# A two-block transformer kernel on one core: the output stages round both weight halves first, two modulation vectors change their place and one its engine

## The reference

```python
# second block, x: 256 x 2048
m = jax.nn.silu(c) @ w_ada + b_ada           # w_ada: 2048 x 6*2048
sh_a, sc_a, g_a, sh_m, sc_m, g_m = split(m)  # and the same of c_ctx for the context
h  = rms_norm(x, norm_attn_w) * (1 + sc_a) + sh_a
hc = rms_norm(ctx, norm_attn_w) * (1 + csc_a) + csh_a
...                                          # keys and values of hc and h, queries, pooling
x = x + g_a * (concat([attn, pool]) @ w_out)
hm = rms_norm(x, norm_mlp_w) * (1 + sc_m) + sh_m
x = x + g_m * (square(relu(hm @ w_up)) @ w_down)
return rms_norm(x, final_norm_w)
```

## Time and profile before

| what | value |
|---|---|
| time before, median of 3 runs | 1773.1 us (1772.69 to 1774.19) |
| the profiled execution | 1774.28 us |
| its span, first to last instruction | 1772.4 us |
| mean granted TensorE clock | 0.971 |
| PE busy | 1635.3 us, 92% |
| DVE busy | 1165.5 us, 66% |
| ACT busy | 768.3 us, 43% |
| raw loads | 496 of 512 KB |
| `w_ada` loads | 64 from SP, 32 from ACT, 1024 KB each |

### The profile page before, as it was taken

The page is one execution under the profiler, slowest core; times in us unless marked ns, Lnnn a source line. Parts: engine busy times, 40 slices in busy tenths (PEclk is TensorE's granted clock), DMA queues, the critical chain, the costliest instruction groups (busy, mean ns, idle before and its releaser), DMA issues.

```text
span 1772.4 us, 33734 instructions
## 1 busy us (share of the span) xinstructions
PE 1635.3 (92%) x12254; PEld 1501.3 (85%) x12254; DVE 1165.5 (66%) x1798; ACT 768.3 (43%) x1067; POOL 32.0 (2%) x49
## 2 busy tenths in 40 slices
PE   3799999899969977998989889999999999999996
PEld 3799998799968867877878879989998999899985
DVE  4577776688885557576755566656665666566675
ACT  4344443344433334444434445434543454345542
POOL 0000000000000000000000010000000000000000
PEclk9899999899989999999999989999999999999998
DMA  7688787688848765762224445555555556555552
GB/s 298 245 277 293 282 289 243 233 318 334 318 169 323 277 242 186 296 254 92 76 84 152 147 151 184 185 188 189 180 188 189 188 179 187 189 184 186 180 190 92
DMA packets 88120, 374.74 MB, mean 211 GB/s; under 512 B 9985, under 2 KB 10513, under 8 KB 75233
## 3 DMA queue, kind: packets, MB, share of 16 engines
q1 hardware_dynamic: 82224, 335.97, 55.3%
q10 hardware_dynamic: 4608, 33.56, 5.2%
q0 software_dynamic: 1200, 4.02, 0.7%
HBM read 371.40 MB, written 2.10 MB: 211 GB/s over the span
## 4 chain that ended last, share of the span: by engine, by line
issue 71%; DVE 12%; PE 11%; ACT 5%; DVEq 1%; POOL 0%; ACTq 0%; POOLq 0%
DVE lo L1088 5%; ACT hi L755 2%; PE G L396 2%; PE G L397 2%; PE G L398 2%; PE ADA L438 1%; PE M L636 1%; ACT sq L934 1%; DVE sqsum L1088 1%; DVE blk L1088 1%; PE S L610 1%; DVE sm L1413 1%; PE S L623 1%; PE ADA L650 1%; ACT actA L946 0%
## 5 line engine op out<-in xcount | busy, mean ns | idle before, releaser
L1088 DVE TENSOR_TENSOR lo<-raw,hi 128x1024 fp32r<-128x1024 f32 x496 | 607.8, 1225 | 326.1 <-ACT hi L755 316.0
L755 ACT ACTIVATE hi<-raw 128x1024 fp32r<-128x1024 f32 x496 | 526.1, 1061 | 488.1 <-PE G L398 276.4
L396 PE MATMUL G<-actA,hi 128*128 128x256 f32 (+1 forms) x2368 | 685.2, 289 | 20.1 <-DVE actA L1088 19.5
L397 PE MATMUL G<-actA,lo 128*128 128x256 f32 (+1 forms) x2368 | 672.5, 284 | 0.0
L398 PE MATMUL G<-actA,hi 128*128 128x256 f32 x2368 | 672.2, 284 | 0.0
L396 PEld LDWEIGHTS G<-actA,hi 128*128 128x128 f32 x2368 | 452.8, 191 | 54.5 <-issue 39.7
L397 PEld LDWEIGHTS G<-actA,lo 128*128 128x128 f32 x2368 | 452.4, 191 | 0.4
L398 PEld LDWEIGHTS G<-actA,hi 128*128 128x128 f32 x2368 | 451.6, 191 | 0.0
L422 PE MATMUL G<-actB,hi 128*128 128x512 f32 x1024 | 355.2, 391 | 0.0
L423 PE MATMUL G<-actB,lo 128*128 128x256 f32 x1024 | 287.2, 281 | 0.0
L422 PEld LDWEIGHTS G<-actB,hi 128*128 128x128 f32 x1024 | 191.6, 187 | 41.4
(11 more groups left out here) (186 smaller groups left out, 1102.1 us busy)
## 6 DMA issues: line engine op xcount, KB each, us to landing
raw<-stream_dram SPq DMA_DIRECT2D x496, 512.0 KB, 3.5
ada_raw<-w_ada_dram SPq DMA_DIRECT2D x64, 1024.0 KB, 6.7
ada_raw<-w_ada_dram ACTq DMA_DIRECT2D x32, 1024.0 KB, 6.4
x_tok<-x_tok_dram SPq DMA_DIRECT2D x1, 2048.0 KB, 8.2
resid<-xT_dram SPq DMA_DIRECT2D x1, 2048.0 KB, 11.7
ctx_tok<-ctx_tok_dram SPq DMA_DIRECT2D x1, 2048.0 KB, 18.5
W<-ctxT_dram POOLq DMA_DIRECT2D x16, 128.0 KB, 5.5
out_dram<-resid SPq DMA_DIRECT2D x4, 512.0 KB, 2.6
```

What stands on the lines that cost most here:

```text
L396: pe.matmul(wide, hi[:, slot, cols], x[:, k, 0:T + extra], start=(k == 0), stop=False, skip_group_check=True)
L397: pe.matmul(wide, lo[:, slot, cols], x[:, k, 0:T + extra], start=False, stop=False, skip_group_check=True)
L755: return act.activation(dst, src, ACT.Copy)
L1088: return dve.tensor_tensor(dst, a, b, op)
```

## The change

**ScalarE's order in the output stages.** In `out_body` the rounding of a unit's second half moves from the end of the unit's work to directly behind the first half. `ada_copy` of `sc_m` behind the first output stage goes.

**`sc_m`.** Its 16 tiles leave the first output stage and take the place that `g_m` had in key and query units, three of them earlier: one behind each of the units `U_KV+1` to `U_KV+7`, four in each of the pairs s = 0 and 1, one in s = 2. The table `SCALE_LOADS` places their loads. ACT copies the sums at the end of pair 2, where it was in pair 3. The turn and the addition that stood in the key units go.

**`g_m`.** PE has no tiles of it any more. DVE sums it in the down units of the MLP's groups 0 and 1: behind every second unit one multiply-add of 128x2048 (`scalar_tensor_tensor` into `gate_part`), 16 in all, from the two slots of `ada_raw`. SP loads each tile as 128x4x512 out of four column blocks (runs of 2 KB in place of 8 KB), and behind each such load the next four halves of weights. PE sums over the partitions ahead of group 3 with 16 matmuls (`gate_sums`), and DVE adds the bias. POOL clears `gate_part` after the first unit of the second output stage.

The diff, cut to its core:

```diff
+SCALE_LOADS = {U_KV + 2: 1, U_KV + 3: 1, U_KV + 4: 1, U_KV + 5: 1, U_KV + 6: 1, U_KV + 7: 2,
+               U_Q: 2, U_Q + 1: 2, U_Q + 2: 2, U_Q + 3: 1}
...
+    "dve gate down": {"seq": 4, "lo_done": 8, "gate_taken": 2},
...
         diag, adas = W[:, 3328:3584], W[:, 3584:4096]
+        gate_part = W[:, 1024:3072]
+        gate_c = cpad[:].rearrange("p k n -> p (k n)")
         ctx_raw = W[:, 0:1024].rearrange("p (s t) -> p s t", s=4)
...
                     ada_load(4 * KT + 1, 1, ada_taken, 2 * KT)
-                elif U_OUT1 <= u < U_KV - 2:
-                    e = u - U_OUT1 + 2
-                    ada_load(4 * KT + e, e % 2, ada_used, 2 * KT + e - 1)
                 weight(2 * u % RING, 2 * u + 8)
                 weight((2 * u + 1) % RING, 2 * u + 9)
-            ada_load(5 * KT, 0, ada_used, 3 * KT)
-            ada_load(5 * KT + 1, 1, ada_used, 3 * KT)
             e = 2
             for u in range(U_KV, U_OUT2):
-                for _ in range(1 if U_KV + 4 <= u < U_Q else 2 if U_Q <= u < U_Q + 6 else 0):
-                    if e < KT:
-                        ada_load(5 * KT + e, e % 2, ada_used, 3 * KT + e - 1)
-                        e += 1
+                for _ in range(SCALE_LOADS.get(u, 0)):
+                    ada_load(4 * KT + e, e % 2, ada_used, 2 * KT + e - 1)
+                    e += 1
                 weight(2 * u % RING, 2 * u + 8)
                 weight((2 * u + 1) % RING, 2 * u + 9)
-            with sp.Fori(0, (2 * UNITS - 2 * U_OUT2 - 8) // RING) as i:
-                for j in range(RING):
-                    weight(j, i * RING + 2 * U_OUT2 + 8 + j)
+            def weights(first, last):
+                with sp.Fori(0, 2 * (last - first) // RING) as i:
+                    for j in range(RING):
+                        weight(j, i * RING + 2 * first + 8 + j)
+            def gate_load(k):
+                m, g = divmod(k, 4)
+                src = ada_w[5 * KT:6 * KT].rearrange("(n m) p (g c) -> m g p n c", m=4, g=4)[m, g]
+                if k > 1:
+                    sp.wait_ge(gate_taken, 1 * (k - 1))
+                sp.dma_start(ada_raw[:, k % 2], src).then_inc(gate_full[k % 2], 16)
+            at = U_OUT2
+            for g in range(2):
+                weights(at, U_MLP + 2 * KT * g + KT)
+                if g == 0:
+                    sp.wait_ge(pool_ready, 4)
+                    gate_load(0)
+                for i in range(8):
+                    if 8 * g + i + 1 < KT:
+                        gate_load(8 * g + i + 1)
+                    at = U_MLP + 2 * KT * g + KT + 2 * i
+                    for n in range(2 * at + 8, 2 * at + 12):
+                        weight(n % RING, n)
+                at += 2
+            weights(at, UNITS - 4)
...
-            pool.wait_ge(ada_used, 4 * KT)
+            pool.wait_ge(ada_used, 2 * KT + KT)
             pool.dma_start(pool_w, t_in["pool_w"]).then_inc(pool_in, 16)
+            pool.wait_ge(w_used, 2 * U_OUT2 + 2)
+            pool.memset(gate_part, 0.0).then_inc(gate_zero, 1)
             power(14)
...
             for n in range(UNITS_OUT):
-                unit(At(U_OUT1), n, actB, inB, ada=2 * KT + n)
+                half_unit(At(U_OUT1), n, 0, actB, inB)
+                if n == 0:
+                    ada_turn()
+                half_unit(At(U_OUT1), n, 1, actB, inB)
                 if n == 1:
...
             broadcast()
             half_unit(at, 1, 1, actC)
+            ada_rows(2 * KT)
             unit(at, 2, actC)
-            ada_turn()
+            ada_rows(2 * KT + 1)
             unit(at, 3, actC)
+            ada_rows(2 * KT + 2)
             turn_values(y2[:, 0], U_KV + 3, 8)
             unit(at, 4, actA, inA, KT)
-            ada_rows(3 * KT)
+            ada_rows(2 * KT + 3)
             turn_values(y2[:, 1], U_KV + 4, 9)
             unit(at, 5, actA)
-            ada_rows(3 * KT + 1)
+            ada_rows(2 * KT + 4)
             pe.wait_ge(blk2_in, 64)
             rotate(y2[:, 0], U_KV + 5)
             unit(at, 6, actA)
-            ada_rows(3 * KT + 2)
+            ada_rows(2 * KT + 5)
             rotate(y2[:, 1], U_KV + 6)
             unit(at, 7, actA)
-            ada_rows(3 * KT + 3)
+            ada_rows(2 * KT + 6)
             turn_values(y2[:, 0], U_KV + 7, 10)
...
-                    pe.wait_ge(ada_added, 3 + 1)
+                    pe.wait_ge(ada_added, 2 + 1)
...
                 if s < 3:
-                    ada_rows(3 * KT + 4 + 4 * s)
-                    ada_rows(3 * KT + 5 + 4 * s)
+                    ada_rows(2 * KT + 7 + 4 * s)
+                if s < 2:
+                    ada_rows(2 * KT + 8 + 4 * s)
                 half_unit(at, 2 * s + 1, 0, actA)
...
                 half_unit(at, 2 * s + 1, 1, actA)
-                if s < 3:
-                    ada_rows(3 * KT + 6 + 4 * s)
-                    ada_rows(3 * KT + 7 + 4 * s)
+                if s < 2:
+                    ada_rows(2 * KT + 9 + 4 * s)
+                    ada_rows(2 * KT + 10 + 4 * s)
...
+            def gate_sums():
+                pe.wait_ge(gate_taken, KT)
+                for m in range(KT):
+                    x = pe.matmul(S[0][:, m:m + 1], gate_part[:, m * P:(m + 1) * P], ones[:, 0:1], start=(m == 0), stop=(m == KT - 1),
+                                  skip_group_check=True)
+                x.then_inc(gate_summed, 1)
...
                 base = U_MLP + 2 * KT * g
+                if g == MLP_GROUPS - 1:
+                    gate_sums()
                 if g == 0:
...
                     split(at, j, 0)
+                    split(at, j)
                     if ctx_too:
...
                     square(at, j, (sq[:, j % 2:j % 2 + 1], resid[:, u]))
-                    split(at, j)
...
                 out_body(At(U_OUT1, 4, i), i, True)
-            ada_copy(2)
...
                 split(at, 2 * s + 1)
+                if s == 2:
+                    ada_copy(2)
                 if s == 0:
...
-                    ada_add(3, 5)
+                    ada_add(2, 4)
...
                     dve.wait_ge(acc_zero, 1)
-                if g < MLP_GROUPS - 1:
+                if g < 2:
+                    if g == 0:
+                        dve.wait_ge(gate_zero, 1)
+                    with turn.lap(dve, 4, "dve gate down") as i:
+                        for j in range(4):
+                            down(At(base + KT, 4, i), j, bass.ds(i * 4 + j, 1), True, None)
+                            if j % 2:
+                                slot = j // 2
+                                dve.wait_ge(gate_full[slot], i * 16 + 16 * (4 * g + 1))
+                                dve.scalar_tensor_tensor(gate_part, ada_raw[:, slot].rearrange("p k n -> p (k n)"),
+                                                         gate_c[:, bass.ds(i * 76 + (8 * 38 * g + 38 * slot + 6), 1)], gate_part,
+                                                         ALU.mult, ALU.add).then_inc(gate_taken, 1)
+                                own(gate_taken)
+                elif g < MLP_GROUPS - 1:
                     with turn.lap(dve, 8, "dve down") as i:
...
                 else:
+                    dve.wait_ge(gate_summed, 1)
+                    seq(tt(adav[:, 0, G_M:G_M + KT], S[0][:, 0:KT], col("b_ada", 5 * KT, KT), ALU.add))
                     with turn.lap(dve, 7, "dve last down") as i:
```

More of the change, by code:

```diff
@@ L237, in program @@
         inP = sem("inP")
+        gate_zero, gate_taken, gate_summed = (sem(n) for n in ("gate_zero", "gate_taken", "gate_summed"))
+        gate_full = [sem(f"gate_full{i}") for i in range(2)]
         out_ready, out_sent = sem("out_ready"), sem("out_sent")
@@ L1010, in _ @@
                     value_copy(V2[:, :, P:T], 12)
-                if s == 3:
-                    ada_copy(3)
                 if s:
@@ L1395, in _ @@
                 split(at, n, 0)
-                if n == 4:
-                    ada_add(2, 4)
                 split(at, n)
```

## The result

The changed kernel takes **1722.8 us** (median of 5, 1722.0 to 1726.5) beside 1772.7 of the kernel before: ratio 0.972, 95% interval 0.971 to 0.974. The forecast was 1714 in a range of 1707 to 1726. The direction and nearly all of the gain are there; 8 to 9 us are missing. The profiled execution took 1722.0 us, its span is 1719.9, its mean granted clock 0.976.

The account below looks back on a forecast made before the run. PE is full nearly everywhere, but in both output stages ACT and DVE waiting for each other hold it. -35.2 - 4.5 - 22.9 + 3.5 = -59.1 gives 1715.2, taken as 1714 us; range 1707 to 1726, held 8 in 10.

Parts of the forecast that it names:

- Part 1: First output stage: ScalarE's new order and 16 tiles gone bring the first key unit's sums to 623.4, -35.2 us.
- ring: Output stages: ACT and DVE wait for each other once a unit, in laps of 7.65 and 6.88 us.
- the wait of 5.54: First key unit: PE stands 5.54 us for the last context tile; forecast to go.
- Part 2: Key and query units: moving the `sc_m` tiles there gives -4.5 us, at worst -2.
- the turn in pair 3: Query units: PE's 2.33 us wait there for ACT's copy goes, as the copy comes a unit earlier.
- Part 3: Second output stage: ScalarE's new order gives 5.75 us a unit and sums at 1007.0, -22.9 us.
- Part 4: MLP down units: `g_m` multiply-adds on VectorE of 2.33 us cost 0; PE's `gate_sums` cost +3.5 us.
- Part 5: Down units: gate loads cost 0, taking 2 KB runs at half a 4 KB run, DMA share 0.90.
- 1 MB ahead of it adds 3.3 at 300 GB/s: Down units: a weight load landing in 3.5 us is delayed 3.3 by a gate tile, within 8.7 of spare.
- The second rival: Down units: the gate's loads delay weights, from 0.14 us a 2 KB run; 1724 to 1749 us; 9%.
- The prediction's own sign of being wrong: PE pausing in down units of groups 0 and 1 with `raw` loads named, or output-stage pitch staying over 6.
- the lower bound: Down units: 512 runs of 2 KB take 53 us of DMA engine time, half that of 4 KB runs.

Follow-up runs that it names:

- adds_only: Changed kernel with no gate loads; the 16 multiply-adds run on whatever stands in the buffers: 1715.8 us, ratio 0.967.
- tiles_8k: Changed kernel, same `g_m` values, its 16 tiles laid out in HBM as one 8 KB run per partition: 1717.0 us, ratio 0.968.
- first_apart: Changed kernel with the first two gate loads moved forward into the up units, four units apart: 1718.2 us, ratio 0.967.
- all_three: Changed kernel with gate tiles in 8 KB runs, first two gate loads four units apart, and `acc` cleared ahead of the power: 1715.7 us, ratio 0.967.
- changed_again: The changed kernel itself once more, on the chip of the run beside it: 1723.1 us, ratio 0.971.
- vectors_only: Changed kernel with ScalarE's old order in the output stages; the modulation vectors still move: 1780.4 us, ratio 1.004.
- loads_only: Changed kernel with all gate loads kept, each multiply-add cut to 16 columns from 2048: 1724.2 us, ratio 0.972.
- runs_8k: Changed kernel with each gate load read as one 8 KB piece a partition, so `g_m` values differ: 1717.2 us, ratio 0.968.
- acc_early: Changed kernel with GpSimd clearing `acc` ahead of its power for the MLP's norm, not behind: 1721.5 us, ratio 0.970.

## Why the prediction was right, and where not

- **Part 1, the first output stage**: right, and to the size: sums at 623.46, forecast 623.4. Units of 5.75, no ring, the wait of 5.54 gone. Both edits are in it: the order alone brought the sums to 644.82, and the tiles, taken out behind it, the other 21.4 us.
- **Part 2, `sc_m`**: forecast -4.5, found -6.0 up to unit 1 of the second output stage. In its own places it gave -4.3: -0.7 in the key units, -3.6 in queries up to the row at 798.45 (837.96 before), and the turn in pair 3 has no wait. The other 1.7 lies behind that, in pairs whose work didn't change, at a granted clock of 0.96 (800 to 875) where it was 0.93 (840 to 916). No run tests why.
- **Part 3, the second output stage**: forecast -22.9. 1029.92 - 915.28 = 114.64 has become 965.88 - 874.08 = 91.80: -22.8. Behind it something was missed: PE waits 2.27 us for the broadcast where it waited 0.23 (at 1036.20). The chain is as long as it was, 5.9 us beside 6.3 from sums to broadcast; but PE, which then ran at the lower clock, now has used up the unit's first half sooner. "The chain runs over POOL and DVE as before" was right and still not free. It is offset in part by less time at the lower clock: adds_only and tiles_8k, which have no pause, stand +4.6 against before in the MLP, 3.6 of it the sums.
- **Part 4, the multiply-adds and the sums**: right. The multiply-add takes 2.35 us (forecast 2.33), `gate_sums` 3.63 (3.5), and adds_only shows no cost on VectorE. What wasn't foreseen is the lower clock behind the sums in some executions, 2 to 3 us by estimate (first_apart stands 1.9 over tiles_8k, all_three above).
- **Part 5, the loads**: this is the step that failed. "Cost 0" measured +6.9 (5.2 in changed_again). What failed is "1 MB ahead of it adds 3.3 at 300 GB/s". Ahead of the first weights stand both tiles, 2 MB, and they move at 220 GB/s (mean of the first two windows): 9.5 us, more than the 8.7 of spare that the same sentence worked out. The weights, forecast to land in 3.5 + 3.3 = 6.8 us, took 11.3 to 15.8. The second rival is what happened, at one place out of sixteen and at less than its lower bound of 10 us. The prediction's own sign of being wrong came up too: PE pauses in the down units of group 0, and the wait behind it leads back to `raw`. 1722.8 still lies inside the stated range because the loss stayed at one place.
- **Part 5, the steady laps**: no pause and a share of 0.90 (1260 to 1340), forecast 0.90, but that agreement is luck. By the packet records of that stretch a 2 KB run took 0.162 us in the mean, not the 0.103 of the lower bound and above the 0.14 from which the rival was to begin; a 4 KB packet took 0.167 where the kernel before had 0.205. The two errors cancel: 3085 x 0.162 + 3858 x 0.167 = 1144 us in 80 x 16. Weights there landed in up to 9.5 us, over the 6.8 and the 8.7, without a pause.
- **The width.** The prediction's terms of 3, 3, 2 and 1 make 9 added up and 4.8 as a root of squares; its 1708 to 1721 is neither. 1722.8 lies outside it and inside the stated 1707 to 1726.

The Trainium skill (DMA: Bandwidth & Descriptors, "Why small descriptors are slow (HBM only)") has by its overhead a 2 KB run at 51% of a 4 KB one. The trace agrees for the packets that meet no delay: half of the 2 KB runs took 0.084 us or less, and a 4 KB packet mostly 0.159, which is 53%. It doesn't for the mean, 0.148 us in the burst and 0.162 in the steady laps, which is what a sum of engine time needs. Why a part of the short runs took several times as long, and those of the third tile didn't, stays open.

The sum, by its parts: -35.2, -6.0, -22.8, and +11.6 in the MLP (3.6 sums, 6.9 first pair, 1.1 for the rest: the wait at the broadcast, less what the clock gave back) is -52.4, the spans' 1772.4 - 1719.9 = 52.5.

## What to carry to other kernels

When two engines wait for each other once a unit, reorder first: work taken from a third engine inside such a ring mostly lengthens its wait (16 tiles were worth 2.2 us here), and the same work pays after the ring is gone (21.4 us). Cost a stream of new loads not only in its steady lap but at its first issue, where all its buffers are free and everything is sent at once: bytes in that burst by the measured rate of its run length, against the spare time of what queues behind. Laying a tile out as one run for each partition, or sending the first two earlier and apart, cured it here; either was worth some 5 to 6 us of 1723.

## What the hardware showed beyond the forecast

- Two 1 MB tiles read in runs of 2 KB out of rows of 8 KB moved at 200 to 240 GB/s with the DMA engines 0.88 to 0.96 busy; with the same values laid out in runs of 8 KB, it was 414 to 416 GB/s and 1.01 to 1.02 over the same 8 us.
- In the changed kernel the mean time of a 2 KB run was 0.15 to 0.18 us in 15 of the 16 tiles and 0.085 in the third, with a median of 0.084 to 0.098 in all.
- A `tensor_scalar` of VectorE from and to SBUF (two of 128x128) takes 0.48 us, and 3.51 us beside a GpSimd clearing of 3.50 us: it began 0.14 us behind the clearing (968.19, 968.05) and ended 0.15 behind it. The Trainium skill (SBUF — State Buffer, "Who interferes with whom") says that a `tensor_scalar` can take both port pairs of VectorE, one of which it shares with GpSimd, and that whichever of the two comes first then blocks the other for its whole instruction. The trace agrees; which ports were used it doesn't show.
- The granted clock fell behind 32 one-column matmul instructions (3.6 to 4.4 us in which PE counts as busy) in vectors_only, loads_only, runs_8k, first_apart, acc_early and all_three, to 0.83 to 0.89 (0.66 in all_three) in the slice of 10 us with its lowest value, and not behind the same ones in tiles_8k, adds_only and both executions of the changed kernel. After the same short waits at 970 it fell in one execution of the changed kernel and not in the other, nor in runs_8k. Why it falls in one execution and not in another stays open.
